# A hybrid attention trunk: x loaded transposed, its roots by matmul, the forget block in the first pass, gate columns moved into pair 0

## The chip, the cores and the metric

The kernel runs on one core of a Trainium2 chip. The metric is device time of one execution in microseconds (us). The core has PE (matmul), DVE (vector), ACT (scalar functions), POOL (general) and SP, which here only issues DMAs.

## The reference

One layer: x (1024 tokens by 1024 features) is normalised, scaled and shifted by columns that a product of silu(c) with w_ada gives, and projected to q, k, v of 16 heads, a gate path and 8 forget logits. Half of the heads do stick-breaking attention, half softmax attention with forget gates. The outputs are normalised, gated, projected by w_out and added to x, and the sum is normalised.

```python
    ada = c_act @ w_ada[layer] + b_ada[layer]
    shift, scale, gate = jnp.split(ada, 3, axis=-1)
    h = rmsnorm(x, g_norm[layer]) * (1.0 + scale[:, None, :]) + shift[:, None, :]
    z = h @ w_in[layer]
    q_sb, k_sb, v_sb, q_fx, k_fx, v_fx, g_path, f_logit = jnp.split(z, split_points, axis=-1)
    ...
    x = x + (1.0 + gate[:, None, :]) * (y @ w_out[layer])
return rmsnorm(x, g_final)
```

## The kernel before

Every engine runs its own list of instructions, written out by hand; semaphores tie them. Two stages matter here.

**The opening.** h is needed with features on the partitions, as h_hi + h_lo (a rounded part and the rest, so that three fast products stand for one exact one). SP loads x as eight tiles of 128 tokens (L424, L428). ACT squares each with a running sum (L743), DVE turns four sums into inverse roots (L961 to L969), and ACT, DVE and POOL multiply the tiles by them. The work then goes by *pieces*: a piece is one chunk d of 128 features by one half th of the tokens, in the order of `first_pieces`: early pieces (0, d) and late ones (1, d), alternating from the fourth on. For each piece PE transposes four 128x128 blocks of x into PSUM (L1329), ACT writes h_hi with scale and shift (L757), ACT or DVE writes the same unrounded into `spare` (L763, L1043), POOL subtracts to get h_lo (L636), and PE multiplies with the split weights of q, k and v of pair 0 (L1352, L1353, L1357). The scale and shift of chunk d are two *columns*, each a DVE reduction of a 128x1024 tile of w_ada against silu(c) (L1014). SP loads those tiles into seven slots in turn (L421). DVE also casts the first weights (L999). After the pieces PE multiplies the forget block for each half, and DVE reduces the eight *gate columns* 16 to 23 (L1014 again), four before and four after the first scores, and then SP stores the gate (L434).

**The attention loop.** There are 8 pairs of heads, each with 16 *steps* (one head and one block of 128 queries). In step g of pair p PE does half a projection unit for the next pair, scores of step g + 2, values, and transposes of step g's probabilities (L1410). ACT takes sigmoids (L822, L823), DVE scans (L1094) and writes the low part of the transposed probabilities (L1154), POOL multiplies (L653) and splits weights (L578, L584). SP loads the next weight block when the step number is a multiple of four (L412); in step 0 that is the key block of pair 1, which stands behind the gate store in SP's list. Transposes use two PSUM banks, freed by L1154.

## Time and profile before

| | us |
|---|---|
| median of 3 runs | 793.72 |
| lowest, highest | 792.29, 795.7 |
| the profiled execution | 790.59 |
| its span, first to last instruction | 788.8 |
| PE busy | 716.6 (91%) |
| DVE busy | 494.2 (63%) |
| ACT busy | 409.4 (52%) |
| POOL busy | 396.7 (50%) |

The profiled execution lies 1.8 us above its span and 3.1 us below the median. In the timeline a row gives a start, a duration, the engine, the line, output and inputs, and in brackets how long the engine had stood idle and what released it. Durations of neighbouring matmuls overlap; the distance of their starts tells what one costs.

### The profile page before, as it was taken

The numbers are of one execution on the slowest core, as the hardware profiler recorded it, in microseconds if no ns is written. First come the engines' busy times: TensorE is split into PE (matmuls) and PEld (weight loads), VectorE is DVE, ScalarE is ACT, GpSimd is POOL, SyncE is SP. The second block draws the span as 40 slices with busy tenths as digits, with TensorE's granted clock in tenths as the row PEclk, the third lists the DMA queues.
The fourth block names the chain that finished last, engine by engine and source line by source line (L and its number), as shares of the span: only waits on it lengthen the run. The fifth ranks groups of instructions, "written<-read, shape, count | busy, mean of one in ns | idle before, by whom it ended". The sixth has DMA issues, their size and how long they took to land.

```text
span 788.8 us, 10998 instructions
## 1 busy us (share of the span) xinstructions
PE 716.6 (91%) x3936; PEld 600.0 (76%) x3936; DVE 494.2 (63%) x996; ACT 409.4 (52%) x848; POOL 396.7 (50%) x322
## 2 busy tenths in 40 slices
PE   0498779889999998999999899999998998999995
PEld 0376567778888887888888788888887887888884
DVE  3865956775565477656554866565567655645566
ACT  4523535675466564646675546457554557423222
POOL 4445406526878454467865535766566464221100
PEclk9999989999999999999999999999999999999999
DMA  8832410022334311023443001244331229792223
GB/s 348 323 108 80 134 27 28 27 82 95 107 108 144 110 55 39 1 95 107 147 148 106 27 27 53 78 154 144 133 114 51 64 91 346 220 325 99 81 89 125
DMA packets 34518, 91.57 MB, mean 116 GB/s; under 512 B 4248, under 2 KB 5912, under 8 KB 33952
## 3 DMA queue, kind: packets, MB, share of 16 engines
q1 hardware_dynamic: 27072, 70.56, 26.0%
q0 software_dynamic: 5376, 14.68, 5.9%
q10 hardware_dynamic: 2016, 5.63, 1.8%
q8 instruction: 32, 0.52, 0.3%
q14 instruction: 22, 0.18, 0.1%
HBM read 67.23 MB, written 23.63 MB: 115 GB/s over the span
## 4 chain that ended last, share of the span: by engine, by line
PE 59%; DVE 14%; ACT 9%; POOL 6%; issue 6%; DMA 5%; ACTq 0%; DVEq 0%; SPq 0%; POOLq 0%
PE psum L1446 10%; PE psum L1352 9%; PE psum L1357 9%; PE psum L1353 9%; PE psum L1434 7%; PE psum L1410 6%; DVE pt_lo L1014 3%; PE psum L1381 3%; DVE work L1094 3%; PE psum L1380 3%; DVE stacks L1062 3%; DMA w_raw<-in_w_blocks 2%; PE psum L1419 2%; DVE pt_lo L1154 2%; DMA w_f_raw<-in_w_f 2%
## 5 line engine op out<-in xcount | busy, mean ns | idle before, releaser
L1352 PE MATMUL psum<-h_hi,w_hi 128*128 128x512 f32 x496 | 208.2, 420 | 9.9 <-DVE stacks L1062 6.3
L1357 PE MATMUL psum<-h_hi,w_lo 128*128 128x512 f32 x496 | 196.4, 396 | 0.0
L1353 PE MATMUL psum<-h_lo,w_hi 128*128 128x512 f32 x496 | 195.3, 394 | 0.0
L653 POOL TENSOR_TENSOR work<-work 128x127 f32<-128x127 f32 (+3 forms) x64 | 79.4, 1242 | 169.0 <-DVE work L1094 169.0
L855 ACT ACTIVATE pt_hi<-psum 128x512 fp32r<-128x512 f32 (+1 forms) x192 | 87.6, 490 | 116.7 <-PE psum L1410 113.2
L1154 DVE TENSOR_TENSOR pt_lo<-psum,pt_hi 128x512 fp32r<-128x512 f32 (+1 forms) x192 | 100.6, 551 | 60.9 <-ACT pt_hi L855 59.4
L1094 DVE TENSOR_TENSOR_SCAN work<-work 128x128 f32<-128x128 f32 (+3 forms) x64 | 103.2, 1614 | 33.5 <-ACT work L823 33.4
L1352 PEld LDWEIGHTS psum<-h_hi,w_hi 128*128 128x128 f32 x496 | 94.9, 191 | 28.6 <-issue 9.2
L1357 PEld LDWEIGHTS psum<-h_hi,w_lo 128*128 128x128 f32 x496 | 94.2, 190 | 21.8
L1353 PEld LDWEIGHTS psum<-h_lo,w_hi 128*128 128x128 f32 x496 | 94.9, 191 | 16.1
L659 POOL TENSOR_SCALAR work<-work,small 128x128 f32<-128x128 f32 (+3 forms) x64 | 47.8, 747 | 91.7 <-DVE small L1117 91.5
L1410 PE MATMUL psum<-ident,work 128*128 128x128 f32 x576 | 87.8, 279 | 5.9 <-POOL work L653 4.0
L584 POOL TENSOR_TENSOR w_lo<-w_raw,w_hi 128x1024 fp32r<-128x1024 f32 x30 | 82.0, 2735 | 9.3 <-DVE w_hi L999 6.9
L827 ACT ACTIVATE work<-work,small 128x128 f32<-128x128 f32 (+3 forms) x64 | 49.8, 778 | 64.4 <-DVE small L1112 64.1
L1434 PE MATMUL psum<-pt_hi,v_stack 128*128 128x256 f32 x320 | 81.1, 288 | 0.3
L1434 PE MATMUL psum<-pt_lo,v_stack 128*128 128x256 f32 x320 | 75.6, 283 | 0.0
L1380 PE MATMUL psum<-stacks 128*128 128x512 f32 (+1 forms) x192 | 66.1, 345 | 7.1 <-DVE mask_bf L1205 3.0
L1125 DVE TENSOR_TENSOR work<-psum,spare 64x256 f32<-64x256 f32 x64 | 26.7, 417 | 71.8 <-ACT spare L836 55.9
L836 ACT ACTIVATE spare<-psum 64x256 f32<-64x256 f32 x64 | 24.3, 380 | 91.2 <-PE psum L1434 90.9
L1410 PEld LDWEIGHTS psum<-ident,work 128*128 128x128 f32 x576 | 62.6, 142 | 8.0 <-POOL work L653 6.1
L1381 PE MATMUL psum<-stacks 128*128 128x512 f32 (+1 forms) x192 | 63.8, 345 | 0.0
L1434 PEld LDWEIGHTS psum<-pt_hi,v_stack 128*128 128x128 f32 x320 | 61.9, 194 | 0.8 <-DVE pt_lo L1154 0.8
(154 smaller groups left out, 1279.6 us busy)
## 6 DMA issues: line engine op xcount, KB each, us to landing
w_raw<-in_w_blocks SPq DMA_DIRECT2D x29, 512.0 KB, 4.2
work<-in_w_ada_t SPq DMA_DIRECT2D x18, 512.0 KB, 4.8
w_split_scratch<-work SPq DMA_DIRECT2D x16, 512.0 KB, 3.0
work<-in_x SPq DMA_DIRECT2D x12, 512.0 KB, 6.6
y_split_scratch<-work SPq DMA_DIRECT2D x10, 512.0 KB, 3.6
work<-forget_scratch SPq DMA_DIRECT2D x8, 512.0 KB, 5.0
work<-in_w_out SPq DMA_DIRECT2D x16, 256.0 KB, 3.1
stacks<-y_split_scratch POOLq DMA_DIRECT2D x4, 1024.0 KB, 6.8
```

The source lines that it names most:

```text
L584: nc.gpsimd.tensor_tensor(lo, raw_of(b), hi.bitcast(fp32), ALU.subtract).then_inc(s_wlo, 1)
L653: nc.gpsimd.tensor_tensor(U[g % 2][:, 0:n - 1], U[g % 2][:, 0:n - 1], R[g % 2][:, 1:n], ALU.mult).then_inc(s_prob, 1)
L855: nc.scalar.activation(pt_hi[:, a:e, (g % 2) * P:(g % 2 + 1) * P], bank, ACT.Copy).then_inc(s_thi, 1)
L1094: nc.vector.tensor_tensor_scan(R[g % 2][:, 0:n][:, ::-1], R[g % 2][:, 0:n][:, ::-1], R[g % 2][:, 0:n][:, ::-1], 1.0, ALU.mult, ALU.bypass) ...
L1154: nc.vector.tensor_tensor(pt_lo[:, a:e, q0:q0 + P], bank, pt_hi[:, a:e, q0:q0 + P].bitcast(fp32), ALU.subtract).then_inc(s_tfree, 1)
L1352: nc.tensor.matmul(bank, hi, h_hi[:, c_, cols], start=(c_ == 0), stop=False)
L1353: last = nc.tensor.matmul(bank, hi, h_lo[:, c_, cols], start=False, stop=(kind == "f" and c_ == DC - 1))
L1357: last = nc.tensor.matmul(bank, lo, h_hi[:, c_, cols], start=False, stop=(c_ == DC - 1))
L1380: nc.tensor.matmul(bank[:, 0:c1 - c0], q, stacks[:, p % 2, a, 1, c0:c1], start=True, stop=False)
L1381: last = nc.tensor.matmul(bank[:, 0:c1 - c0], q, stacks[:, p % 2, a, 2, c0:c1], start=False, stop=not diagonal)
L1410: last = nc.tensor.transpose(bank[:, (k - a) * P:(k - a + 1) * P], U[g % 2][:, k * P:(k + 1) * P], ident[:])
L1434: last = nc.tensor.matmul(OUT[:, c0:2 * P], v_stack[:, p % 2, a, k, :], src[:, k, c0:2 * P], start=(k == 0 and n == 0), stop=(k == qb + 1 ...
```

## The change

- The host passes x a second time, transposed: half, chunk, 128 features, 512 tokens. SP loads it into `work` and `x_late`, two chunks a DMA. PE's transposes of x are gone.
- Squares: ACT squares a chunk (128x512) into one of two buffers, and PE sums over the partitions by four matmuls against a column of ones, accumulating over the chunks. DVE makes the inverse roots as before, multiplies the identity by them, PE spreads them to all partitions with one fp32 matmul against a square of ones, and ACT copies the result to `roots`.
- A piece: DVE scales x by column and roots into `spare`, ACT adds the shift into h_hi, DVE computes h_lo. POOL has no part in it. The first casts of w go from DVE to ACT.
- PE's first pass has four blocks, the forget block among them: 11 matmuls a piece instead of 9 (11 = 4 x hi by h_hi, 3 x lo by h_hi, 4 x hi by h_lo). The hi products are issued when h_hi is there, the products with h_lo after.
- Columns are reduced in place. The eight gate columns go to DVE's steps 1 to 8 of pair 0, their loads into two slots, the last six in SP's steps 1 to 6; the gate is stored in step 9. The key block of pair 1 is then no longer behind it.
- Loads: the k and v weights move from ACT's queue to SP's, behind the first two column tiles.

```diff
-    units = [(p, kind, h) for h in range(NHALF) for p, kind in blocks[:N_FIRST - 1]]
-    units += [(-1, "f", h) for h in range(NHALF)]
+    units = [(p, kind, h) for h in range(NHALF) for p, kind in blocks[:N_FIRST]]
...
+        v_stack, (x_late,) = sb_with_early("v_stack", [P, 2, 2, TB, P], [[P, DC, HALF]])
+        pt_hi, (x_sq, root_diag) = sb_with_early("pt_hi", [P, TB, 2 * P], [[P, 2, HALF], [P, 2, HALF]])
+        pt_lo, (roots,) = sb_with_early("pt_lo", [P, TB, 2 * P], [[P, 2, HALF]])
...
+        SUM_BANK = (0, 7)
+        ROOT_BANK = (1, 6)
...
-            for t in range(4):
-                sp.dma_start(x_tile(t), x_tiles[t]).then_inc(s_x[t], 16)
-            for n in range(6):
+            for j in range(4):
+                load_x(0, j)
+            for n in range(2):
                 load_ada(n)
-            for t in range(4, TB):
-                sp.dma_start(x_tile(t), x_tiles[t]).then_inc(s_x[t], 16)
-            for n in range(6, 3 * DC):
+            sp.dma_start(w_early[:, 0], w_block(0, "k")).then_inc(s_wearly[0], 16)
+            sp.dma_start(w_early[:, 1], w_block(0, "v")).then_inc(s_wearly[1], 16)
+            for n in range(2, 4):
                 load_ada(n)
-                if n == 2 * DC - 1:
-                    load_w(N_FIRST)
-            sp.wait_ge(s_gate, 1)
-            sp.dma_start(gate_dram.rearrange("a (b p) -> p (a b)", p=P), a_cols,
-                         allow_slow_non_contiguous=True).then_inc(s_gst, 16)
+            for j in range(4):
+                load_x(1, j)
+            for n in range(4, 2 * DC):
+                load_ada(n)
+            load_w(N_FIRST)
+            for n in range(2 * DC, 2 * DC + LATE_SLOTS):
+                load_ada(n)
...
+                if p == 0 and GATE_FROM <= i < GATE_FROM + DC - LATE_SLOTS:
+                    load_ada(2 * DC + LATE_SLOTS + i - GATE_FROM)
+                if p == 0 and i == GATE_FROM + DC:
+                    store_gate()
...
-            for n in range(2 * DC):
-                h_lo_piece(n)
-                if n == 2:
-                    split_w(3)
+            for b in range(N_FIRST):
+                split_w(b)
...
+            def x_squares(th):
+                for d in range(DC):
+                    n = th * DC + d
+                    if d % 2 == 0:
+                        act.wait_ge(s_x[n // 2], 16)
+                    if n >= 2:
+                        act.wait_ge(s_xsum, n - 1)
+                    nc.scalar.activation(x_sq[:, n % 2, :], x_tile(th, d), ACT.Square).then_inc(s_xsq, 1)
...
+            split_first_w(0)
+            x_squares(0)
+            split_first_w(1)
             x_roots(0)
-            normalise_x(0, [2])
+            split_first_w(2)
+            roots_down(0)
+            split_first_w(3)
             for n in range(2 * DC):
-                if n in (1, 2):
-                    x_squares(2 * n + 2)
-                    x_squares(2 * n + 3)
-                if n == 3:
+                if first_pieces[n] == (0, 2):
+                    x_squares(1)
+                if first_pieces[n] == (1, 0):
                     x_roots(1)
-                    normalise_x(1, [6, 7])
+                    roots_down(1)
                 h_piece(n)
...
+                nc.vector.scalar_tensor_tensor(out=spare[:, n % 2, :], in0=x_tile(th, d), scalar=a_cols[:, d:d + 1],
+                                               in1=roots[:, th, :], op0=ALU.mult, op1=ALU.mult).then_inc(s_xscaled, 1)
...
+                nc.vector.scalar_tensor_tensor(out=h_lo[:, d, cols], in0=spare[:, n % 2, :], scalar=ada[:, d:d + 1],
+                                               in1=h_hi[:, d, cols].bitcast(fp32), op0=ALU.add,
+                                               op1=ALU.subtract).then_inc(s_hlo, 1)
...
+            for n in range(2, 2 * DC):
+                if first_pieces[n] == (1, 0):
                     x_roots(1)
-                    normalise_x(1, [4, 5])
-                h_piece(n)
-            for n in range(2 * DC, 2 * DC + 4):
-                ada_column(n)
...
+                scale_x(n)
+                if first_pieces[n][0] == 0 and first_pieces[n][1] + 1 < DC:
+                    columns(first_pieces[n][1] + 1)
+                h_lo_piece(n)
...
+                if p == 0 and GATE_FROM <= i < GATE_FROM + DC:
+                    ada_column(2 * DC + i - GATE_FROM)
...
+            def sum_x_squares(th):
+                for d in range(DC):
+                    pe.wait_ge(s_xsq, th * DC + d + 1)
+                    for t in range(4):
+                        last = nc.tensor.matmul(psum[:, SUM_BANK[th], t:t + 1],
+                                                x_sq[:, d % 2, t * P:(t + 1) * P], ones,
+                                                start=(d == 0 and t == 0), stop=(d == DC - 1 and t == 3))
+                    last.then_inc(s_xsum, 1)
+            def spread_roots(th):
+                pe.wait_ge(s_diag, th + 1)
+                nc.tensor.matmul(psum[:, ROOT_BANK[th], :], ones_square[:], root_diag[:, th, :], start=True,
+                                 stop=True).then_inc(s_rdown, 1)
...
+            for n in range(2 * DC):
+                if first_pieces[n] == (0, 2):
+                    sum_x_squares(1)
+                if first_pieces[n] == (1, 0):
+                    spread_roots(1)
+                first_piece(n)
```

On PE, at the end of piece 1 of the opening. Before (the transposes fetch a coming piece, the rest is the pass over q, k and v):

```order
L1357 MATMUL psum<-h_hi,w_lo 128x512
L1352 MATMUL psum<-h_hi,w_hi 128x512
L1353 MATMUL psum<-h_lo,w_hi 128x512
L1357 MATMUL psum<-h_hi,w_lo 128x512
L1352 MATMUL psum<-h_hi,stacks 128x512
L1353 MATMUL psum<-h_lo,stacks 128x512
L1357 MATMUL psum<-h_hi,stacks 128x512
L1329 MATMUL psum<-ident,work 128x128 x4
```

and in the changed kernel (h_hi, h_lo: parts of h; pt_hi_early_52: the buffers of squares; stacks: split weights of v and the forget block):

```order
L1364 MATMUL psum<-h_hi,stacks 128x512
L1375 MATMUL psum<-h_lo,w_hi 128x512 x2
L1375 MATMUL psum<-h_lo,stacks 128x512 x2
L1339 MATMUL psum<-ones,pt_hi_early_52 128x1 x32
L1364 MATMUL psum<-h_hi,w_hi 128x512
L1366 MATMUL psum<-h_hi,w_lo 128x512
L1364 MATMUL psum<-h_hi,w_hi 128x512
L1366 MATMUL psum<-h_hi,w_lo 128x512
```

The 32 sums of squares of the second half stand between piece 1 and piece 2, where only transposes stood.

On DVE, one round of a late and an early piece. Before (L1043 writes `spare` from PSUM, ISA rows are columns and the reads of their sums):

```order
L1043 TENSOR_SCALAR spare<-psum,small 128x512 [waits s_hlo,s_hhi]
L1014 ISA pt_lo,small<-stacks_early_50,work 128x1024 [waits s_ada,s_wa3]
L1014 ISA small 128x1
L1014 ISA pt_lo,small<-stacks_early_50,work 128x1024 [waits s_ada,s_wa4]
L1014 ISA small 128x1
L1023 TENSOR_TENSOR small<-small 128x1 [waits s_ada]
L1024 SCALAR_TENSOR_TENSOR small<-small 128x1
L1043 TENSOR_SCALAR spare<-psum,small 128x512 [waits s_hlo,s_hhi]
```

and in the changed kernel (L1045 scales, L1053 makes h_lo, pt_lo_early_54 is `roots`):

```order
L1045 SCALAR_TENSOR_TENSOR spare<-v_stack_early_51,small,pt_lo_early_54 128x512 [waits s_hlo,s_acol,s_rall]
L1053 SCALAR_TENSOR_TENSOR h_lo<-spare,small,h_hi 128x512 [waits s_hhi]
L1045 SCALAR_TENSOR_TENSOR spare<-work,small,pt_lo_early_54 128x512 [waits s_hlo,s_acol,s_rall]
L1021 ISA stacks_early_50,small<-stacks_early_50,work 128x1024 [waits s_wa3]
L1021 ISA small 128x1
L1021 ISA stacks_early_50,small<-stacks_early_50,work 128x1024 [waits s_wa4]
L1021 ISA small 128x1
L1028 TENSOR_TENSOR small<-small 128x1 [waits s_ada]
L1029 SCALAR_TENSOR_TENSOR small<-small 128x1
L1053 SCALAR_TENSOR_TENSOR h_lo<-spare,small,h_hi 128x512 [waits s_hhi]
```

A round had one large operation beside its columns, and now has four of two SBUF inputs, two of which wait for ACT (s_hhi).

On DVE, steps 2 and 3 of pair 0. Before:

```order
L1154 TENSOR_TENSOR pt_lo<-psum,pt_hi 128x3x128 [waits s_thi]
L1094 SCALAR_TENSOR_TENSOR work<-work 128x640 [waits s_sig]
L1154 TENSOR_TENSOR pt_lo<-psum,pt_hi 128x4x128 [waits s_thi]
L1094 SCALAR_TENSOR_TENSOR work<-work 128x768 [waits s_sig]
L1073 SCALAR_TENSOR_TENSOR stacks<-psum,stacks 64x512 [waits s_phi]
L1073 SCALAR_TENSOR_TENSOR stacks<-psum,stacks 64x512
```

and in the changed kernel (L1021 is a gate column, L1165 the low part of the probabilities, L1105 the scan):

```order
L1021 ISA v_stack_early_51,small<-v_stack_early_51,work 128x1024 [waits s_wa8]
L1021 ISA small 128x1
L1165 TENSOR_TENSOR pt_lo<-psum,pt_hi 128x3x128 [waits s_thi]
L1105 SCALAR_TENSOR_TENSOR work<-work 128x640 [waits s_sig]
L1021 ISA v_stack_early_51,small<-v_stack_early_51,work 128x1024 [waits s_wa7]
L1021 ISA small 128x1
L1165 TENSOR_TENSOR pt_lo<-psum,pt_hi 128x4x128 [waits s_thi]
L1105 SCALAR_TENSOR_TENSOR work<-work 128x768 [waits s_sig]
```

A gate column stands ahead of each step's low part of the probabilities.

## Rows read from the trace of the kernel before

**Rows 1.** The page, part 2: busy tenths in 40 slices of 19.7 us.

```profile
PE   0498779889999998999999899999998998999995
...
POOL 4445406526878454467865535766566464221100
```

**Rows 2.** Waits of PE, 18 to 240 us: engine line waited for, total, times, longest.

```profile
PE psum L1329 <- DVE work L986: 20.6, 1, 20.6
PE psum L1401 <- DVE work L1083: 6.3, 1, 6.3
...
PE psum L1329 <- ACT v_stack_early L770: 5.2, 1, 5.2
```

**Rows 3.** Timeline, 38 to 105 us: start us, us, engine line op out<-in, [idle before].

```profile
38.94 0.78 PE L1352 MATMUL psum<-h_hi,w_hi 128*128 128x512 f32 x1
...
86.23 1.39 DVE L1073 SCALAR_TENSOR_TENSOR stacks<-psum,stacks 64x512 fp32r<-64x512 f32 x2
...
93.29 1.37 DVE L1014 CUSTOM_DVE_ANT_0 pt_lo<-work 128x1024 fp32r<-128x1024 f32 x1
...
99.21 2.79 DVE L1062 TENSOR_TENSOR stacks<-psum,stacks 64x512 fp32r<-64x512 f32 x4
...
104.19 0.77 PE L1352 MATMUL psum<-h_hi,w_hi 128*128 128x512 f32 x1
```

**Rows 4.** Timeline, 54 to 62 us: one round of the x pieces.

```profile
54.30 0.81 DVE L1043 TENSOR_SCALAR spare<-psum,small 128x512 f32<-128x512 f32 x1 [2.24 <-ACT h_hi L757]
...
55.02 1.21 DVE L1014 CUSTOM_DVE_ANT_0 pt_lo<-stacks_early,work 128x1024 fp32r<-128x1024 f32 x1
...
55.18 2.20 POOL L636 TENSOR_TENSOR h_lo<-spare,h_hi 128x512 fp32r<-128x512 f32 x1 [0.25 <-DVE spare L1043]
...
56.16 2.30 DVE L1014 CUSTOM_DVE_ANT_0 pt_lo<-stacks_early,work 128x1024 fp32r<-128x1024 f32 x1
...
58.89 0.78 ACT L757 ACTIVATE h_hi<-psum,small 128x512 fp32r<-128x512 f32 x1 [4.63 <-DVE small L1024]
...
61.04 0.81 DVE L1043 TENSOR_SCALAR spare<-psum,small 128x512 f32<-128x512 f32 x1 [2.25 <-ACT h_hi L757]
```

**Rows 5.** DVE by line and shape, whole run: count, busy us, mean ns, idle before.

```profile
L1302 DVE SCALAR_TENSOR_TENSOR work<-work,small 128x512 f32<-128x512 f32 x2 | 1.4, 748 | 0.0
...
L1203 DVE CAST ident_bf<-ident 128x128 bf16<-128x128 f32 x1 | 0.2, 226 | 0.0
```

**Rows 6.** ACT by line and shape, whole run.

```profile
L757 ACT ACTIVATE h_hi<-psum,small 128x512 fp32r<-128x512 f32 x16 | 12.4, 777 | 33.8 <-DVE small L1024 29.2 <-PE psum L1329 4.5
...
L743 ACT ACTIVATE pt_hi<-work 128x1024 fp32r<-128x1024 f32 x4 | 4.2, 1054 | 3.0 <-DMA work<-in_x 3.0
...
L869 ACT ACTIVATE pt_hi<-work 128x512 fp32r<-128x512 f32 x2 | 1.3, 631 | 1.8 <-DVE work L1280 1.8
```

**Rows 7.** The sums of squares of one pair, line 1419: min/median/max ns, first and last start.

```profile
L1419 PE MATMUL psum<-ones,work x16: 222/250/250, 211.9 to 213.6; 128*128 128x1 f32 x16
```

**Rows 8.** Chain of waits: start us, spacing us, what; projection matmuls at two spacings.

```profile
42.70 0.43 PE psum L1357
...
45.11 0.23 PE psum L1353
```

**Rows 9.** DMA, 0 to 40 us in 40 slices of one us.

```profile
GB/s 0 61 210 216 329 420 414 419 392 427 410 418 426 399 396 410 401 414 410 414 401 414 410 414 401 414 410 414 401 410 414 414 401 410 406 107 4 0 0 0
```

**Rows 10.** Timeline, 103 to 124 us: the load of the key weights and its users.

```profile
103.84 17.61 SPq L412 DMA_DIRECT2D w_raw<-in_w_blocks  x2
...
117.56 1.05 POOL L578 TENSOR_SCALAR w_hi<-w_raw 128x1024 fp32r<-128x1024 f32 x1 [4.52 <-DMA w_raw<-in_w_blocks]
...
123.38 0.66 PE L1410 MATMUL psum<-ident,work 128*128 128x128 f32 x4 [1.62 <-POOL work L653]
```

**Rows 11.** Waits, 104 to 190 us, pair 0.

```profile
DVE pt_lo L1154 <- ACT pt_hi L855: 11.3, 8, 4.3
...
DVE work L1094 <- ACT work L823: 8.3, 10, 1.2
```

More of the change, by code:

```diff
@@ L908, in _ @@
             scores_out(1)
-            for u in range(4, 2 * N_FIRST):
+            for u in range(N_FIRST, 2 * N_FIRST):
                 proj_out(u)
@@ L1026, in norm_columns @@
                                                op0=ALU.add, op1=ALU.mult).then_inc(s_acol, 1)
-            for b in range(N_FIRST):
-                split_first_w(b)
             dve.wait_ge(s_const, 16)
@@ L1418, in sum_squares @@
                 for t in range(TB):
-                    last = nc.tensor.matmul(bank[:, t:t + 1], squares[:, t * P:(t + 1) * P], ones[:], start=True, stop=True)
+                    last = nc.tensor.matmul(bank[:, t:t + 1], squares[:, t * P:(t + 1) * P], ones, start=True, stop=True)
                 last.then_inc(s_t, 1)
```

264 lines of the change are left out of this document (124 added, 140 removed).

## Prediction

> **What bounds the kernel now.** I read the page's tenths and PE's waits first, then the timeline of the opening, then the chain of waits. The profiled execution took 790.6 us around a span of 788.8 us. From pair 1 on PE is busy nine tenths of nearly every slice [rows 1], and this change touches nothing there, so what it can move is the time at which the attention loop starts and what pair 0 costs. PE idles 20.6 us until the first x tiles are normalised, 5.2 us until the second half is, and 6.3 us before the loop [rows 2]. The loop's first projection matmul starts at 104.19 us [rows 3].
>
> Between 45 and 78 us the x pieces come in rounds of a late and an early piece, 61.04 - 54.30 = 6.74 us each [rows 4]. The reader is to see one chain in them: DVE copies a piece out (0.7 us to the next start), reduces two adaLN columns (55.02 to 58.46, 3.44 us, because the second takes 2.30 where the first took 1.21: POOL's h_lo runs beside it for 2.20 us), closes the column pair, and then waits 2.25 us for three operations of ACT [rows 4]. PE's share of such a round is 18 matmuls at 0.23 us and eight transposes, about 5 us, so the DVE to ACT chain bounds it, not PE. Then comes a tail: DVE starts the copies out of the projections at 86.23 us and the loop starts 17.96 us later, of which 93.29 to 99.21 us, 5.9 us, are four gate columns [rows 3].
>
> **The change, part by part.**
>
> *First roots.* ACT now takes the casts of w (about 1.05 us each, by the Square of the same width) and eight squares of half the width, 0.63 us each without the accumulator read [rows 6]. DMA has the first half of x, c and the query weights (3.2 MB) in at about 10 us, and the key weights, ninth in line, at about 14 us, adding up the row of rates [rows 9]; I put the query weights at 8.6, so ACT ends their cast at 9.7, the squares at 9.7 + 8 x 0.63 = 14.7, the key cast at 15.9, and the roots are there at about 17.3. Four diagonal tiles at 0.15 to 0.23 us by the small cast [rows 5] give 18.1; before, the first transposes started at 20.6 [rows 2]. Then PE spreads the roots by one fp32 matmul of 512 columns. No row has such a one: the bounds are 0.23 and 0.43 us, the two spacings of a projection matmul of that width [rows 8], if it costs one of those, and four of them, 0.9 to 1.7 us, if the unsplit operands cost what a split product in parts would; I take the dear end, 1.7 us at the slow start, because nothing here excludes it, and 20.5 us for the end of ACT's copy. The Trainium skill ("FP8 and Floating Point Precision", section TensorE Precision Notes) says that true FP32 takes four passes; by it the matmul would be 4 x 0.43 = 1.7 us, and by one pass 0.43. The price falls twice. Meanwhile DVE reduces the first two columns, 2.6 to 3.5 us, so the first scaled piece starts at 22.0 and ACT's h_hi of it ends near 23.5. Pieces 0 and 1 so come some us earlier than before.
>
> *Second roots.* Here the change adds a wait. On ACT the eight squares of the second half stand ahead of h_hi of piece 2, and on PE their sums stand behind the last matmuls of piece 1. With two buffers, squares 3 to 8 can't run before PE sums. DVE has h_lo of piece 1 at about 30.2 (scale 0.75, columns 2.6, h_lo 0.75, twice, by the two-input row of 0.748 [rows 5]); PE ends piece 1 at 31.2. Four sums cost 4 x 0.11 = 0.5 us [rows 7], less than ACT's 0.63, so six squares take about 4.5 us to 35.7. Then h_hi (0.7) and h_lo (0.75) of piece 2 to 37.2, the root chain 1.5, diagonals 0.7, spread 0.9 at the faster rate, copy 0.65: DVE scales the first late piece at 41.1. Before, PE began that piece at 38.94 [rows 3]. At the slower rate (0.43 against 0.23 [rows 8]) sums, piece 2 and spread add 4 to 5 us.
>
> *Rounds.* POOL leaves the pieces, so a column should cost 1.21 us instead of 2.30. A round becomes scale 0.75, wait for ACT 0.8 (0.63 to 0.78 for one operation [rows 6]), h_lo 0.75, scale 0.75, columns 2.6, h_lo 0.75, sum 6.4 us. That is only 0.3 us less than 6.74: DVE has gained two-input operations for what POOL and ACT lost. PE now needs 22 matmuls of 0.23, 5.0 us, since the forget block is in the pass, so it still isn't the bound. Four rounds carry columns: 41.1 + 4 x 6.4 = 66.7. The last five pieces have none and cost DVE 5 x 2.3 = 11.5 us (to 78.2) and PE 5 x 2.5 = 12.5 us (to about 81). DVE began its tail at 86.23 before, and now at 78.2: 8.0 us of gain.
>
> *Tail.* The four gate columns of 5.9 us leave it, and so do the two casts of identity and mask (0.5 us, now in DVE's idle start). PE had the late forget blocks to do beside this tail, under cover; they cost nothing there, and moving them costs 2 x 2 matmuls a round, hidden behind DVE as said. What ends last in the new tail is ACT's work on the late units, which the gate columns partly hid. From 78.2: DVE's early q and k 4.2 us (1.39 + 2.79 [rows 3]), scores and sigmoids 2.1, ACT's late q 1.2 (two half copies at the 0.6 of a full-width one), DVE's late q 1.4 and k 2.8, the forget copy 0.65, PE's transposes 0.8, handovers 0.35: 13.5 us, where a plain difference would say 17.96 - 6.4 = 11.6. The loop starts at 78.2 + 13.5 = 91.7, which is **12.5 us** earlier.
>
> *Pair 0, the load.* Before, SP issues the load of the key weights of pair 1 only after the gate store, at 103.84, behind a store of scattered words; POOL gets them at 117.56 and is then late with the products, for which PE waits 1.62 us at 123.38 [rows 10]. Now that load is free to go at the loop's start and the store sits in step 9. I credit 1.7 us.
>
> *Pair 0, the columns.* Eight columns of 1.3 us go to DVE's queue in steps 1 to 8, each ahead of the step's copy of transposed probabilities (queued behind it: that copy, which frees PE's transpose banks, and the scan, for which POOL's product and PE's transposes two steps on wait). Their cover is the time in which DVE waits for ACT: 11.3 us in 8 waits and 8.3 us in 10 [rows 11], over 15 steps, some 1.2 us a step. Walking steps 1 to 8 with DVE's own rows, the column ends mostly within 1.4 us of the moment at which the copy was due, and the scan after it again waits for ACT, as before. So the bounds are 0 and 8 x 1.3 = 10.4 us uncovered (18.4 at 2.30 each [rows 4]); I take 2.2 us, nearer the covered end because DVE waits in nearly every step. Their loads, 4 MB in 40 us, meet idle queues: the first two are in long before, the next is issued a step or two ahead.
>
> Sum: 12.5 + 1.7 - 2.2 = 12.0 us. The profiled execution would be 778.6 instead of 790.6, and the median, which stands 3.1 us above it, goes from 793.7 to **781.7 us**.
>
> **Rivals.**
>
> A: the gap of the second roots opens. If PE runs at the slower rate while it sums squares, because its work there is thin, the loop starts 4 to 5 us later: 786 us. For it: PE's matmuls stood 0.43 us apart until 43 us before [rows 8], after just such a broken start. Against: from 23.5 to 31 us PE now has nearly unbroken work.
>
> B: the columns in pair 0 are only half covered, 1 us each beyond the 2.2: 6 us more, 787.5 us. For it: steps 3 and 5 carry a projection copy of 1.4 to 2.8 us and leave DVE less than 1 us.
>
> C: slower than before. One mechanism: in pair 0 each column overlaps a product or split of POOL. Both read two SBUF operands, and a column beside POOL's h_lo took 2.30 instead of 1.21 [rows 4]. Eight columns then take 18.4 us, and POOL's products slow by as much, so that PE waits for them; if none of it is covered, 12.5 + 1.7 - 18.4 = -4.2, that is 798 us. It decides the sign once a step loses more than 14.2 / 8 = 1.8 us. The Trainium skill ("GPSIMD Engine Reference", section Specifications) speaks against the change in this way: GpSimd's SBUF interface is shared with VectorE instructions that have two SBUF inputs. This trace agrees with it (2.30 against 1.21). By that rule a column costs 2.3 us wherever POOL works and 1.2 us elsewhere; POOL is busy four to five tenths of the slices of pair 0 [rows 1], which is why I don't expect it in every step.
>
> D: more gain than I forecast. If the round falls to 5.9 us (SBUF operands read faster than PSUM ones, ACT's wait 0.6) and the second gap to 38 us, 12.0 + 2 + 3 = 17: 776.7 us.
>
> E: the early start is given back, because something with a clock of its own ends the opening: the adaLN columns' loads. 8 MB of them at 0.41 MB a us [rows 9] are in by 36 us, so I give it little; it would leave 790 us or more, no change.
>
> **How the numbers follow.** Chances: the forecast (778 to 785) 0.46; A 0.16; B 0.13; D 0.14; E or B and A together, within 0.5% (789.8 to 797.7), 0.07; C 0.04. A measurement of this kernel can tell about 0.5%, 4 us, from no change. The range takes in A, B and most of D and reaches 774 to 789: it leaves out C, E and D's far end. Faster by over 0.5%: 0.46 + 0.16 + 0.13 + 0.14 = 0.89. Same: 0.07. Slower: 0.04.
>
> **What would show it.** In the profile of the changed kernel: the first h_hi ends at about 23.5 us; the first late piece is scaled at about 41; then DVE's scalings of late pieces lie 6.4 us apart, with columns of 1.2 us each and no 2.3 among them once POOL has split w; the loop's first projection starts at 91.7 us; the key weights are split before step 1's product is due, and PE has no wait of 1.6 us on POOL in step 3; steps 1 to 8 last as long as before within 0.5 us. It would be wrong if the rounds hold 6.7 us or more (two-input operations on DVE dearer than 0.75), if ACT's squares crawl behind PE's sums (over 0.9 us each), or if pair 0 lengthens by more than it gains.

## The result and the profile after

The changed kernel takes 798.68 us (median of 7 runs, 796.76 to 802.03) against 793.8 us before (7 runs, 791.9 to 795.7): a ratio of 1.0057, 95% interval 1.0035 to 1.008. It is slower by 0.6%, where I had predicted 781.7 us and a range of 774 to 789. The profiled execution has a span of 796.6 us, against 788.8. These 7.8 us are more than the 4.9 us between the medians: the profiled execution before lay 3.1 us under the median of its three runs, and the one after stands at its median. Part of what the two traces differ by is therefore not the change.

From the page after, the tenths of PE and POOL, which answer [rows 1]:

```profile
PE   4689879789999998999999999999998998999995
POOL 2200135426869453467875535766566465221100
```

From the twelfth slice on PE is about as full as it was. POOL has almost nothing to do in slices 3 and 4, where it made h_lo before. The loss must be in the opening and in what tenths don't show.

PE's waits up to 180 us (engine and line waited for, us in total, times, longest), which answer [rows 2]:

```profile
PE psum L1339 <- ACT pt_hi_early L757: 10.0, 1, 10.0
PE psum L1440 <- DVE work L1094: 6.9, 1, 6.9
PE psum L1364 <- ACT h_hi L785: 5.1, 5, 2.2
PE psum L1347 <- DVE pt_hi_early L1002: 4.6, 1, 4.6
PE psum L1449 <- POOL work L666: 3.2, 1, 3.2
```

PE starts earlier than before (9.96 instead of 20.6 us), but with sums of squares and not with the projections. The timeline shows what that is worth. Columns: start us, duration us, engine, line, operation, out<-in, count, and in brackets the idle time ahead and who ended it. ACT's squares of the first half:

```profile
9.21 1.13 ACT L757 ACTIVATE pt_hi_early<-work 128x512 f32<-128x512 f32 x2
11.90 0.63 ACT L757 ACTIVATE pt_hi_early<-work 128x512 f32<-128x512 f32 x1 [1.56 <-PE psum L1339]
13.54 0.63 ACT L757 ACTIVATE pt_hi_early<-work 128x512 f32<-128x512 f32 x1 [1.01 <-PE psum L1339]
...
20.37 0.63 ACT L757 ACTIVATE pt_hi_early<-work 128x512 f32<-128x512 f32 x1 [1.02 <-PE psum L1339]
```

A square takes 0.63 us as forecast, but there are two buffers, and once both are full squares follow each other only every 1.7 us, as fast as PE sums. DVE, through the first roots to the first scaled piece:

```profile
23.86 0.16 DVE L992 TENSOR_SCALAR small<-psum 128x4 f32<-128x4 f32 x1 [14.69 <-PE psum L1339]
...
25.36 2.92 DVE L1002 TENSOR_SCALAR pt_hi_early<-ident,small 128x128 f32<-128x128 f32 x4
...
31.08 0.75 DVE L1045 SCALAR_TENSOR_TENSOR spare<-work,small,pt_lo_early 128x512 f32<-128x512 f32 x1 [0.18 <-ACT pt_lo_early L767]
```

And the second roots and the rounds, again DVE (the first late piece, and two later ones a round apart):

```profile
56.81 0.75 DVE L1045 SCALAR_TENSOR_TENSOR spare<-v_stack_early,small,pt_lo_early 128x512 f32<-128x512 f32 x1 [4.51 <-ACT pt_lo_early L767]
...
62.96 0.75 DVE L1045 SCALAR_TENSOR_TENSOR spare<-v_stack_early,small,pt_lo_early 128x512 f32<-128x512 f32 x1
...
69.10 0.75 DVE L1045 SCALAR_TENSOR_TENSOR spare<-v_stack_early,small,pt_lo_early 128x512 f32<-128x512 f32 x1
```

On PE the second sums and what follows them:

```profile
40.53 9.35 PE L1339 MATMUL psum<-ones,pt_hi_early 128*128 128x1 f32 x64
49.74 0.77 PE L1364 MATMUL psum<-h_hi,w_hi 128*128 128x512 f32 x1
...
54.58 1.56 PE L1347 MATMUL psum<-pt_hi_early,ones 128*128 128x512 f32 x2
```

The tail begins on DVE at 92.84 us (86.23 before [rows 3]) and the loop's first projection follows at 105.69 (104.19 before [rows 3]):

```profile
92.84 1.39 DVE L1084 SCALAR_TENSOR_TENSOR stacks<-psum,stacks 64x512 fp32r<-64x512 f32 x2 [0.34 <-ACT stacks L808]
...
104.96 1.08 PE L1440 MATMUL psum<-ident,work 128*128 128x128 f32 x4 [6.92 <-DVE work L1094]
105.69 0.78 PE L1394 MATMUL psum<-h_hi,w_hi 128*128 128x512 f32 x1
106.27 0.63 PE L1395 MATMUL psum<-h_lo,w_hi 128*128 128x512 f32 x1
```

So of the 7.8 us by which the span grew, 1.5 are there when the loop starts. Two marks further on are PE's sums of output squares. Those of pair 0 start at 215.8 us after and at 211.9 before [rows 7], 3.9 us later. The last ones (duration ns min/median/max, first and last start us), first after, then before:

```profile
L1458 PE MATMUL psum<-ones,work x16: 203/250/251, 751.0 to 752.7; 128*128 128x1 f32 x16
```

```profile
L1419 PE MATMUL psum<-ones,work x128: 200/250/250, 211.9 to 744.8; 128*128 128x1 f32 x128
```

752.7 - 744.8 = 7.9 us: 4.0 us are lost in pairs where the program is the same. What differs there is the granted clock in some stretches (start and end us, length; busy us of PE, PEld, DVE, ACT and POOL with counts; then PEclk, DMA share and GB/s), first after, then before (which also had 1.00 from 40 to 60 and from 120 to 180):

```profile
40.00:60.00 20.00, 17.78 (x86) 15.07 (x85) 7.44 (x21) 6.12 (x11) 0.00 (x0) 0.72 0.27 85
100.00:120.00 20.00, 15.04 (x68) 12.37 (x69) 11.88 (x20) 8.92 (x20) 6.85 (x5) 0.74 0.10 30
140.00:160.00 20.00, 15.73 (x78) 12.93 (x77) 17.61 (x25) 9.91 (x18) 9.83 (x7) 0.91 0.17 53
160.00:180.00 20.00, 17.81 (x91) 14.28 (x90) 14.25 (x16) 13.67 (x28) 4.44 (x4) 0.91 0.22 82
300.00:320.00 20.00, 17.46 (x91) 14.22 (x89) 14.34 (x21) 7.98 (x19) 7.75 (x7) 0.91 0.05 14
600.00:620.00 20.00, 17.98 (x99) 15.25 (x98) 13.28 (x18) 10.71 (x25) 11.91 (x10) 0.91 0.20 66
```

```profile
100.00:120.00 20.00, 16.55 (x74) 13.56 (x75) 10.04 (x18) 7.16 (x19) 3.22 (x3) 0.83 0.15 26
300.00:320.00 20.00, 18.84 (x101) 15.75 (x102) 13.62 (x18) 9.67 (x24) 7.32 (x6) 1.00 0.08 27
600.00:620.00 20.00, 17.33 (x96) 14.23 (x95) 15.90 (x22) 9.42 (x22) 11.09 (x11) 1.00 0.22 71
```

TensorE has two levels here, 1.2 and 2.4 GHz; a stretch of 20 us with a mean of 0.91 spends 0.09 x 20 x 2 = 3.6 us at the lower one and loses 1.8 us if PE is what is waited for. The changed kernel has more of these. In its opening PE had been summing (rows of one column, L1339) before the clock fell, and at 100 us it had waited 6.9 us; at 300 and 600 us I see no such reason.

### The profile page after: what moved, and what is told of

Read it like the earlier page. It is cut to its first block, busy times and chain, and to the rows that moved or that the text cites. A ratio compares the mean times of both kernels' runs of the same rounds, so it can differ in the third digit from the quotient of the medians.

```text
span 796.6 us, 11108 instructions
## 1 busy us (share of the span) xinstructions
PE 739.4 (93%) x4004; PEld 621.5 (78%) x4004; DVE 496.5 (62%) x1020; ACT 405.6 (51%) x843; POOL 368.3 (46%) x305
## 4 chain that ended last, share of the span: by engine, by line
PE 67%; DVE 11%; ACT 8%; POOL 6%; issue 5%; DMA 2%; DVEq 0%; ACTq 0%; POOLq 0%
PE psum L1485 11%; PE psum L1394 10%; PE psum L1396 9%; PE psum L1395 9%; PE psum L1473 7%; PE psum L1449 6%; PE psum L1420 3%; PE psum L1419 3%; PE psum L1339 3%; DVE work L1105 3%; DVE stacks L1073 2%; DVE pt_lo L1165 2%; POOL work L666 2%; PE psum L1458 2%; ACT work L835 1%
## 5 line engine op out<-in xcount | busy, mean ns | idle before, releaser
L1394 PE MATMUL psum<-h_hi,w_hi 128*128 128x512 f32 x464 | 195.0, 420 | 6.0 <-DVE stacks L1073 6.0
L1396 PE MATMUL psum<-h_hi,w_lo 128*128 128x512 f32 x464 | 185.3, 399 | 0.0
L1395 PE MATMUL psum<-h_lo,w_hi 128*128 128x512 f32 x464 | 184.3, 397 | 0.0
L1165 DVE TENSOR_TENSOR pt_lo<-psum,pt_hi 128x512 fp32r<-128x512 f32 (+1 forms) x192 | 100.7, 552 | 57.3 <-ACT pt_hi L870 55.9
L1105 DVE TENSOR_TENSOR_SCAN work<-work 128x128 f32<-128x128 f32 (+3 forms) x64 | 102.3, 1598 | 29.6 <-ACT work L836 29.4
L1394 PEld LDWEIGHTS psum<-h_hi,w_hi 128*128 128x128 f32 x464 | 89.8, 194 | 22.8 <-issue 7.7
L1396 PEld LDWEIGHTS psum<-h_hi,w_lo 128*128 128x128 f32 x464 | 89.0, 192 | 20.4
L1395 PEld LDWEIGHTS psum<-h_lo,w_hi 128*128 128x128 f32 x464 | 89.4, 193 | 15.7
L612 POOL TENSOR_TENSOR w_lo<-w_raw,w_hi 128x1024 fp32r<-128x1024 f32 x30 | 80.1, 2671 | 9.3 <-ACT w_hi L779 6.9
L606 POOL TENSOR_SCALAR w_hi<-w_raw 128x1024 fp32r<-128x1024 f32 x29 | 35.1, 1211 | 68.3 <-PE psum L1369 62.0
```

What stands on the lines that cost most here:

```text
L1105: nc.vector.tensor_tensor_scan(R[g % 2][:, 0:n][:, ::-1], R[g % 2][:, 0:n][:, ::-1], R[g % 2][:, 0:n][:, ::-1], 1.0, ALU.mult, ALU.bypass) ...
L1165: nc.vector.tensor_tensor(pt_lo[:, a:e, q0:q0 + P], bank, pt_hi[:, a:e, q0:q0 + P].bitcast(fp32), ALU.subtract).then_inc(s_tfree, 1)
L1394: nc.tensor.matmul(bank, hi, h_hi[:, c_, cols], start=(c_ == 0), stop=False)
L1395: nc.tensor.matmul(bank, hi, h_lo[:, c_, cols], start=False, stop=False)
L1396: last = nc.tensor.matmul(bank, lo, h_hi[:, c_, cols], start=False, stop=(c_ == DC - 1))
```

## The experiments

"V" is the start of the first transposes of V, 0.7 us ahead of the loop's first projection. The ratio is to runs of the kernel before on the same chip.

| kernel | V, us | median, us | ratio (95% interval) |
|---|---|---|---|
| before | 103.45 | 793.8 | 1 |
| changed kernel | 104.96 | 798.68 | 1.0057 (1.0035 to 1.008) |
| e1 sums rounded | 95.67 | 788.66 | 0.9934 (0.9907 to 0.996) |
| e2 columns alone | 93.59 | 783.76 | 0.9873 (0.9842 to 0.9903) |
| e3 key load alone | 102.97 | 792.18 | 0.9978 (0.9957 to 0.9999) |
| e4 columns kept in the opening | 125.51 | 815.12 | 1.0282 (1.0226 to 1.0338) |
| e5 squares between pieces | 91.08 | 785.18 | 0.9866 (0.9836 to 0.9896) |
| e6 scale ahead | 89.79 | 783.71 | 0.9855 (0.9815 to 0.9894) |
| e7 gate columns shifted | 89.66 | 785.44 | 0.9869 (0.9832 to 0.9906) |
| e8 PE kept busy | 104.70 | 795.32 | 1.0004 (0.9984 to 1.0025) |
| e9 e6 and busy | 91.32 | 781.38 | 0.9842 (0.9811 to 0.9873) |
| e10 splits after diagonals | 91.22 | 782.87 | 0.9858 (0.9833 to 0.9883) |
| e11 before, kept busy | 103.65 | 794.06 | 1.0004 (0.9978 to 1.003) |

**e1: are the sums the cause?** The changed kernel with squares and ones rounded to the fast matmul format, two columns wide.

```diff
-nc.tensor.matmul(psum[:, SUM_BANK[th], t:t + 1],
-                 x_sq[:, d % 2, t * P:(t + 1) * P], ones, ...)
+nc.tensor.matmul(psum[:, SUM_BANK[th], 2 * t:2 * t + 2],
+                 x_sq[:, d % 2, t * P:(t + 1) * P].bitcast(fp32r), ones_square[:, 0:2].bitcast(fp32r), ...)
```

> The changed kernel with the squares and the ones read as fp32r in the sums of squares (two columns wide, the second one unused); all else as in the change. Theory S (PE's sums of squares made the opening late: an fp32 matmul is two records, 0.43 us at PE's lower rate, four a chunk, 1.65 us against ACT's 0.63): a chunk's sums fall under 0.9 us, ACT's squares follow each other in 0.7 to 0.9 us, the first roots come 6 to 8 us earlier, the first late piece is scaled at 43 to 47 us instead of 56.8, the loop starts at 92 to 96 us instead of 105.7, and the median is 786 to 790 us. Rival L (the loads of x in rows of 2 KB, or the order of the loads, made the roots late): the squares stay as far apart as they are and the median stays at 798 +- 2.

V moved from 104.96 to 95.67, 9.3 us, and the time from 798.7 to 788.7. (The first late piece is scaled at 47.52 us and the loop's first projection starts at 96.41, both about half a microsecond past what theory S gave.) PE's rows:

```profile
9.94 7.22 PE L1339 MATMUL psum<-ones,pt_hi_early 128*128 128x2 f32 x32 [9.94 <-ACT pt_hi_early L757]
```

32 records for 32 matmuls, in 7.2 us instead of 13.8 for 64. An exact sum had twice this price, and it was on the path; rival L falls. With 9.3 of the 14.0 us by which the loop's start missed the forecast (105.69 against 91.7), it is the larger part of the miss, and it is shown. A part of the 9.3 us came with it through the clock, which was 0.88 from 40 to 60 us in e1 and 0.72 in the changed kernel.

**e2: the gate columns alone.** The kernel before, with its eight gate columns, their loads and the gate store moved into pair 0 as in the change; x comes in and is transposed as before. With the store moved, the key load is free too, so e2 holds e3's part as well.

```diff
-            for n in range(2 * DC, 2 * DC + 4):
-                ada_column(n)
+                if p == 0 and GATE_FROM <= i < GATE_FROM + DC:
+                    ada_column(2 * DC + i - GATE_FROM)
```

> The kernel before with one part of the change alone: the eight gate columns reduced in place in steps 1 to 8 of pair 0, their loads and the gate's store moved with them, so that the key weights are loaded at the loop's start. Theory C (DVE's waits cover the columns in the loop): the loop starts 5.9 us earlier, at 98.3 us, pair 0 takes at most 1 us longer than before, and the median is 787 to 790. Rival U (uncovered, because POOL slows the columns and they slow POOL): pair 0 takes 6 to 10 us longer and the median is 793 to 798.

```profile
93.59 0.63 PE L1415 MATMUL psum<-ident,work 128*128 128x128 f32 x4 [2.33 <-DVE work L1099]
130.77 1.97 PE L1424 MATMUL psum<-ident,work 128*128 128x128 f32 x8 [3.24 <-POOL work L671]
```

V comes 9.9 us earlier, not 5.9; DVE's tail begins at 79.07 us in this kernel. Before, DVE reduces four more gate columns ahead of its tail, between 79.6 and 86.2:

```profile
79.61 1.22 DVE L1014 CUSTOM_DVE_ANT_0 pt_lo<-work 128x1024 fp32r<-128x1024 f32 x1
...
86.23 1.39 DVE L1073 SCALAR_TENSOR_TENSOR stacks<-psum,stacks 64x512 fp32r<-64x512 f32 x2
```

Columns of both groups were on the path, for V came 9.9 us earlier, more than either group's 6.6 and 5.9 us. Columns and key load together bring 1.3%, 10 us, most of my whole forecast of 12, and more than theory C's 787 to 790 us. The new cover is good: pair 0 shows one wait of 3.2 us in step 7, and from V to its sums of squares (201.6 us) it takes 108.0 us, against 108.5 before.

**e3: the key load alone.** The kernel before, with the load of pair 1's key weights ahead of the gate store.

```diff
+            load_w(N_FIRST + 1)
             sp.wait_ge(s_gate, 1)
             sp.dma_start(gate_dram...
```

> The kernel before with one DMA moved: the load of pair 1's key weights stands ahead of the gate's store in SP's list instead of behind it. Theory C credits it with the wait of 1.6 us in step 3: POOL splits the key weights before 115 us, PE has no wait on POOL in step 3, median 792 +- 1. Rival: the wait is made up later, or another takes its place (PE waits for ACT or DVE): median 793.8 +- 1.

The wait of 1.6 us in step 3 is gone and the ratio says 0.2%, 1.7 us, with an interval that just leaves out 1. Theory C holds: PE waits for POOL no more in step 3.

**e4: the changed kernel with the gate columns back in the opening**, four ahead of the tail and four behind the first scores, and the store in step 9.

> The changed kernel with the eight gate columns back in DVE's opening, four ahead of the first copies and four behind the first scans, the gate's store still in step 9. Theory C: the loop starts 5.9 us later than in the change, at 111 to 112 us, pair 0 gives back 1 to 3 us, median 801 to 804. Rival U: pair 0 gives back 6 us or more, median 792 to 798.

Both theories missed: 815 us against 801 to 804 and 792 to 798. It says less than hoped, because it brought waits of its own. DVE in that kernel:

```profile
94.45 1.47 DVE L1019 CUSTOM_DVE_ANT_0 v_stack_early<-v_stack_early,work 128x1024 f32<-128x1024 f32 x1 [2.17 <-DMA v_stack_early<-in_w_ada_t]
```

The tiles of w_ada now live in the room of late x, free only after the last scaling, two at a time, so each pair of columns waits for its load (2.17, 2.02, 1.81 and 2.44 us). 20.5 us later at V is the price of columns plus loads. Undoing a part inside the changed kernel was not the same as never having made it; e2 is the clean test.

**e5: the second roots.** On e1: five early pieces ahead of the first late one, and the second half's squares and sums two chunks at a time behind pieces 0 to 3. (With `AHEAD = 5` in `first_pieces`.)

```diff
+                first_piece(n)
+                if n < 4:
+                    sum_x_squares(1, range(2 * n, 2 * n + 2))
```

> On top of the rounded sums (788.7 us): five first-half pieces go ahead of the first second-half piece, and the second half's squares and sums stand two chunks at a time between the first four pieces, not eight in a row ahead of the third. Theory G (the second late step of the opening is the block of second-half squares and sums, in which VectorE waited 3.65, 0.89 and 2.97 us in the run with the rounded sums): those 7.5 us of waits fall to about 1.5, transposes of V start near 90 instead of 95.7, median 781 to 785. Rival T (TensorE's total work ahead of the loop is the bound, 16 pieces at 2.55 us and 128 sum records, so the order is worth nothing): transposes at 94 to 96, median 787 to 790.

V is 4.6 us earlier (91.08), and the median is 785.2, just past theory G's 781 to 785. DVE's waits of 3.65 and 2.97 us are down to under 0.4 each, since it has columns to reduce meanwhile. The order was worth about what theory G said; rival T falls.

**e6: VectorE's order.** On e5: piece n + 1 is scaled ahead of h_lo of piece n.

```diff
+                if n + 1 < 2 * DC and n != AHEAD - 1:
+                    scale_x(n + 1)
                 h_lo_piece(n)
```

> The run before and one more change: VectorE scales piece n + 1 ahead of h_lo of piece n, so that ScalarE's rounding of piece n runs beside it. Theory V (VectorE's chain sets the opening): the waits of 0.79 us on ScalarE, nine of them, go, but the last pieces then run at TensorE's 2.55 us instead of VectorE's 2.2; loop 3 to 5 us earlier, median 777 to 781. Rival T (TensorE is the bound once the squares are out of the way): within 1 us of the run before.

All eleven waits of 0.79 us are gone from DVE, but V is only 1.3 us earlier. Between 60 and 80 us (e5 first, then this kernel):

```profile
60.00:80.00 20.00, 19.78 (x87) 16.40 (x88) 13.11 (x19) 8.09 (x13) 0.00 (x0) 1.00 0.10 30
```

```profile
60.00:80.00 20.00, 20.00 (x90) 16.58 (x89) 16.03 (x23) 11.66 (x17) 0.00 (x0) 1.00 0.16 53
```

PE was already full there in e5. DVE's tail now starts at 72.62 us instead of 78.95, and then DVE waits 5.26 us for ACT's sigmoids, which wait for PE's first scores. Rival T is nearer: once the squares are out of the way, PE's 11 matmuls a piece bound the late rounds, and DVE's waits cost little. The intervals of e5 and e6 overlap, so the 1.5 us between the medians isn't shown.

**e7: the wait in step 7.** On e6: gate columns in steps 1 to 5 and 7 to 9, the store in step 10.

```diff
-        GATE_FROM = 1
+        GATE_STEPS = [1, 2, 3, 4, 5, 7, 8, 9]
```

> The run before and one more change: the gate columns stand in steps 1 to 5 and 7 to 9 of pair 0, none in step 6, where GpSimd splits the gate weights. Theory P (the wait of 3.2 us of TensorE in step 7 is the split and a column of 2.77 us slowing each other): that wait falls to about 1, as in the kernel before, the column in step 7 takes 1.2 us, and the time falls by 1.5 to 3 us. Rival W (the split alone, or a scan beside it, makes the wait): no change, or the wait moves to step 7 or 8.

No gain. POOL in that kernel:

```profile
117.83 2.67 POOL L668 TENSOR_TENSOR work<-work 128x895 f32<-128x895 f32 x1 [4.20 <-DVE work L1107]
120.48 3.02 POOL L608 TENSOR_SCALAR w_hi<-w_raw 128x1024 fp32r<-128x1024 f32 x1
...
168.29 1.05 POOL L608 TENSOR_SCALAR w_hi<-w_raw 128x1024 fp32r<-128x1024 f32 x1 [5.03 <-DMA w_raw<-in_w_blocks]
```

PE's wait in step 7 fell from 3.21 to 2.38 us only. The product of 895 columns took 2.67 us, beside the column of step 5 at 117.68 (1.77 at 161.49, beside none), and the cast took 3.02 us (1.05 elsewhere) without any column beside it. DVE's scan of 1024 columns had started 0.33 us ahead of that cast:

```profile
120.15 2.50 DVE L1107 TENSOR_TENSOR_SCAN work<-work 128x1024 f32<-128x1024 f32 x1 [0.34 <-ACT work L838]
```

The scan ends at 122.65 us, and the cast 0.85 us later. In the kernel before the cast came first (135.48, the scan at 136.24) and took 1.06 us. The cast of this step took 3.02 or 3.03 us in the changed kernel, e2, e6, e7 and e8, each time with the scan of 1024 columns started 0.3 us ahead of it. So rival W is nearer, with its scan: by these rows it is the column of step 5, which delays the product and with it the cast, and not the column of step 6 that starts the trouble. No run moved that column alone. And the store, one step later in SP's list, now held up the next load of weights, so that POOL waited 5.03 us and PE 3.13 us at 173.79. Theory P had about a quarter of the wait.

**e8: does the clock cost time?** The changed kernel with 24 products of 128 x 512 on PE in its wait of 6.9 us; nobody reads them.

```diff
+            for _ in range(24):
+                nc.tensor.matmul(psum[:, 5, :], h_hi[:, 0, 0:P], h_hi[:, 0, 0:HALF], start=True, stop=True)
             transpose_v(0, 0)
```

> The changed kernel with 24 added products of 128 x 512 on TensorE, into a bank nobody reads, in the 6.9 us that it waits ahead of the first transposes of V. They add work and compute nothing. Theory K (the 10.2 us of lower granted clock from 101.4 on are a consequence of that wait, and cost time in the first steps of the loop): transposes of V still start near 105, the granted clock of 100 to 120 us rises from 0.74 to over 0.9, and the median falls from 798.7 by 2 to 5 us. Rival N (the clock there costs nothing, because other engines set the pace): 798 to 799. Rival L (the products run at the lower clock, take over 6.9 us and delay the loop): 800 to 802.

```profile
97.58 5.72 PE L1539 MATMUL psum<-h_hi 128*128 128x512 f32 x24
104.70 0.63 PE L1440 MATMUL psum<-ident,work 128*128 128x128 f32 x4 [1.41 <-DVE work L1094]
...
105.40 0.39 PE L1395 MATMUL psum<-h_lo,w_hi 128*128 128x512 f32 x1
```

```profile
100.00:120.00 20.00, 18.59 (x95) 15.09 (x94) 14.36 (x24) 10.16 (x24) 7.37 (x5) 1.00 0.08 27
```

(The second fence is the stretch from 100 to 120 us.) Clock 1.00 instead of 0.74, the loop's first projections 0.39 us long instead of 0.63, and V where it was. PE's wait on POOL in step 7 ends 2.7 us earlier (141.86 against 144.58), pair 0's sums of squares start 3.4 us earlier (212.4 against 215.8), and the ratio fell from 1.0057 to 1.0004, with intervals that don't meet. So work that nobody reads saved some 4 us in this kernel, most of it in pair 0, where the clock was higher; theory K holds here.

**e9: the same 24 products in e6.**

> The kernel with five pieces ahead and the scale ahead of h_lo, with the 24 added products of the earlier run in the wait ahead of the transposes of V (they compute nothing). Theory K (a wait of TensorE of some 7 us costs the clock after it, whatever the kernel): the lower stretch at the start of the loop, 6.8 us there, goes, transposes of V stay near 90, and the median falls from 783.7 by 2 to 4 us, to 780 to 782. Rival N (what the products gave before came from elsewhere in the loop and not from the start): within 1 us of 783.7.

The lower stretch at the loop's start went, but V came 1.5 us later (91.32). The products did not do that: they ended at 89.69 us, and PE still waited 1.64 us for DVE. PE's first scores had come 1.5 us later (83.38 against 81.89), behind a lower stretch from 40 to 60 us (0.91, where e6 had 1.00). The time is 781.4 against 783.7, with overlapping intervals: as expected in size, not separated from no change. It has the lowest median of the study, 1.6% below the kernel before and about 2% below the changed one, but its interval overlaps that of e2, too.

**e10: who slows the first roots?** On e9: POOL starts its second split only when the first diagonals are made.

```diff
             split_w(0)
+            pool.wait_ge(s_diag, 1)
             for b in range(1, N_FIRST):
```

> The run before and one more change: GpSimd starts the splits of the value, key and forget weights only when VectorE has made the first diagonals. Theory O (VectorE's two products of 128 x 4, 2.03 and 2.26 us instead of 0.16, wait for GpSimd's subtractions of 2.34 us to end): they take 0.16 to 0.2 us each, the diagonals start at 19 instead of 23, the first piece on TensorE starts 2 to 4 us earlier; the columns beside the moved subtractions lose some of it again; median 1 to 3 us lower. Rival Q (the first piece waits for the moved split of the weights instead): transposes of V at the same time as in the run before or later.

DVE's first roots in e6 (in e9 they are the same within 0.2 us), then in e10:

```profile
18.23 2.03 DVE L982 TENSOR_TENSOR small<-small 128x4 f32<-128x4 f32 x1
20.30 2.26 DVE L984 TENSOR_TENSOR small<-small 128x4 f32<-128x4 f32 x1
```

```profile
18.18 0.16 DVE L984 TENSOR_TENSOR small<-small 128x4 f32<-128x4 f32 x1
...
20.90 3.36 DVE L1024 CUSTOM_DVE_ANT_0 work<-work 128x1024 f32<-128x1024 f32 x1
24.30 2.17 DVE L1031 TENSOR_TENSOR small<-small 128x1 f32<-128x1 f32 x1
```

The mechanism is shown and the gain is not there. Two products of four columns cost 0.16 us each once POOL is quiet, and the spread starts at 19.90 us instead of 23.79 in e9; but the subtractions then meet the first two columns (3.36 instead of 1.22) and a sum of one column (2.17 instead of 0.16), and the first projection piece starts at 28.41 us, against 28.09 in e9. That is rival Q in effect, with another victim.

**e11: the 24 products in the kernel before**, in a bank not in use.

> The kernel before with 24 added products of 128 x 512 on TensorE in the 6.3 us that it waits ahead of the first transposes of V (they compute nothing). Theory K: the two lower stretches after 93 us (3.4 and 6.8 us) become shorter, the one at the start of the loop goes, and the median falls from 793.5 to 795.5 by 2 to 4 us. Rival N: no change, 0.998 to 1.002.

Missed: 1.0004. The granted clock was 0.83 from 80 to 100 us and 1.00 from 100 to 120, instead of 0.91 and 0.83: the lower stretch had moved ahead of the products. Another came later (0.91 from 160 to 180, 1.00 before), and PE waited 2.97 us on POOL in step 3 instead of 1.62. PE reached step 3 1.1 us earlier (122.28 against 123.38); a stretch of 0.91 costs up to 1.8 us, and pair 0's sums of squares start at 212.4 us, against 211.9 before. So keeping PE busy is not a rule; in the changed kernel it paid, here not.

## Why the prediction was wrong

Against the forecast the span came out 19.8 us longer (796.6 against 788.8 - 12.0 = 776.8): 14.0 us until the loop starts, 1.9 in pair 0, 4.0 after it. The medians missed by 17.0 us; the other 3 us or so come from the light execution before. The gate columns and the load came out as forecast or better; what failed is the new path of x, and in it first the price of a sum.

**The price of a sum, the step that failed.** I wrote "Four sums cost 4 x 0.11 = 0.5 us [rows 7], less than ACT's 0.63". Rows 7 show 16 records over 1.7 us, and I took them for 16 matmuls. The program has eight there (one for each of eight blocks of tokens): each fp32 matmul of this form leaves two records. The true price was 0.23 us at the faster rate and 0.43 at the slower, so four cost 0.9 to 1.7 us, which is more than ACT's 0.63 at either rate. The second half's squares show the one (0.91 us apart), the first half's the other (1.7). Squares ended at 21.0 and not at 14.7. The check was at hand: count the matmuls in the code against the x of the row. My own list of signs had the danger ("if ACT's squares crawl behind PE's sums, over 0.9 us each"), and yet no rival carried it.

**Contention in the first roots.** Diagonals at 4 x 0.15 to 0.23 us were 2.92 us; in the second half, with POOL idle, 0.88. POOL's row beside the first:

```profile
25.28 2.34 POOL L612 TENSOR_TENSOR stacks<-stacks_early,stacks 128x1024 fp32r<-128x1024 f32 x1 [0.92 <-ACT stacks L779]
```

DVE's four operations started 0.08 us behind it and ended 0.66 us after it. e10 shows this kind of stall directly. The Trainium skill ("SBUF — State Buffer", section Who interferes with whom) says that the port pair shared by VectorE and GpSimd is an exclusive lock: whichever of the two comes first keeps it for its whole instruction, and the other is blocked, not slowed. The traces agree: in e6 a product of four columns started at 18.23 and took 2.03 us, until GpSimd's subtraction (17.90, 2.34 us) had ended. I had used that contention for the columns, by a factor, and not for small operations, to which it adds the rest of the other engine's instruction.

**The spread.** I took the dear end, 1.7 us; it was two records and 2.07 us from start to end (28.34), 0.4 above my upper bound, part of which is the way a matmul's end is recorded (0.63 us long at a spacing of 0.43). The Trainium skill's rule of four passes ("FP8 and Floating Point Precision", section TensorE Precision Notes) gives, as an estimate, 4 x 0.43 = 1.7 us, and 4 x 0.23 = 0.9 us at the faster rate. The traces bear that out better than one pass: 2.07 us here and 1.02 in e6. I weighed the rule here and not at the sums, which are fp32 matmuls too.

**The second roots.** Forecast 41.1, measured 56.81: 9.1 us came over from the first, the sums and squares took 9.2 instead of 4.5, and piece 2 and the spread ran at the lower clock (0.43 apart; 0.72 granted in 40 to 60). The granted clock was 0.50 from 46 to 50 us, while PE was still summing. So rival A's reason, the slower rate during the sums, held for the later part of this gap; it had no part for the sums' price.

**Rounds and tail.** Right: 6.14 us against 6.4, columns 1.22 without a 2.3 among them, ACT's wait 0.79, last five pieces 2.2 us each, tail 12.85 against 13.5. All of it started 14.6 us late.

**The sum's 12.5.** This hid an error in the other direction. By "DVE began its tail at 86.23 and now at 78.2" I booked 8.0 us to the new path of x. But 6.6 us of the kernel before's way to 86.23 were gate columns; with those moved, in e2, the tail begins at 79.07. So with e2's figure my forecast gave the new path of x 79.07 - 78.2 = 0.9 us up to the tail and 93.98 - 91.7 = 2.3 us up to the loop's first projection, and the columns nearly all the rest. With V at 93.59 in e2 and 104.96 in the changed kernel, and the same columns in both, the path of x as written costs 11.4 us. Had I split the sum by parts of the change and not by stages, I would have seen that most of the forecast gain was in the simple part and most of the new costs in the other. Even mended, the new path has not paid: e6 starts V 3.8 us before e2, and the two medians are 783.71 and 783.76.

**Pair 0.** The load: 1.7 credited, 1.6 on the spot and 1.7 by e3. The columns: 2.2 taken; they took 1.2 us each but for 1.80 and 2.77, and PE waited 3.2 us in step 7 (a wait that stands in e2 too). The dear one, and POOL's split beside it:

```profile
139.90 2.77 DVE L1021 CUSTOM_DVE_ANT_0 v_stack_early<-v_stack_early,work 128x1024 f32<-128x1024 f32 x1
```

```profile
139.19 2.39 POOL L612 TENSOR_TENSOR w_lo<-w_raw,w_hi 128x1024 fp32r<-128x1024 f32 x1
```

Up to the sums of pair 0 the loop lost 3.9 - 1.5 = 2.4 us, against 2.2 - 1.7 = 0.5 in my sum. From V to these sums the changed kernel took 110.9 us and the kernel before 108.5, but e8, with the same columns and without the lower stretch at the loop's start, 107.7, and e2 108.0. So the loss in pair 0 was mostly the clock's and not the columns'. Rival C, in which every column meets POOL, did not come true; that its 798 us are what was measured is luck, for the slower result had another cause.

**The clock.** No term for it. After pair 0, where both kernels do the same, the profiled execution of the changed kernel lost 4.0 us. Two more lower stretches (0.91 at 300 and at 600 us, 1.00 before) have 3.6 us between them. From the sums of pair 0 to the last ones, the kernel before and e11, with one lower stretch in that time, took 532.9 and 533.9 us; seven kernels with two took 535.5 to 536.3; and the changed kernel, e5, e6 and e7, with three, 536.1 to 537.1. e3 is among the seven and differs from the kernel before by one DMA. So most of these 4.0 us go with the number of lower stretches and not with the change, and as far as the execution before was a light one they are not in the medians. That the stretches are the cause is read from this order, not from an experiment.

## To carry to other kernels

Before pricing an operation by a row, match the row's count with the number of instructions in the code; an fp32 matmul may stand there as two records, and half the price turned an ACT-bound loop into a PE-bound one. Split a forecast by parts of the change as well as by stages: here one cheap move of work under cover was worth nearly all of the gain, and the large rewrite beside it ate it. Compare what two profiles differ by with what their medians differ by: one execution can lie some microseconds off. Work that goes back and forth between two engines with two buffers runs at the slower of them; put other pieces between, as e5 did. And ask which instruction of the other engine starts first: a delay of 0.9 us put POOL's cast behind a scan instead of ahead of it, and it took 3.0 us instead of 1.1.

## What the runs showed of the hardware

An unrounded fp32 matmul against ones leaves two records: 64 sums left 128, at 0.21 us each where matmuls stood 0.43 us apart, and a spread of 512 columns took 2.07 us, or 1.02 in e6 at the faster rate. A VectorE product of four columns, 0.16 us alone, took up to 2.26 us beside a GpSimd subtraction of 2.34 us. A GpSimd cast of 128x1024 took 1.06 us when it started ahead of VectorE's scan of 1024 columns and 3.02 when it started 0.3 us behind it. Lower stretches of TensorE's clock also came where PE had been busy: near 300 and 600 us in the changed kernel, e5, e6 and e7. e8 and e9, with the 24 added products, had none there and one between 440 and 480 us, and so had e1, e2, e4 and e10, the first three without such products. Why, no run here tells.
